# Attention weights turned by 32x32 blocks on DVE and exchanged through DRAM, in place of TensorE transposes

## Chip, cores and metric

One NeuronCore of a Trainium2 chip. The metric is the device time of one execution in microseconds, lower is better; for the kernel before, three runs gave a median of 1193.29 us (1192.71 to 1195.32).

## What is computed

One hybrid decoder layer on x (1, 1024, 1024) in float32: RMSNorm, a projection to six blocks of 512 columns (conv gate b, c, h and attention q, k, v), a causal 3-tap convolution on four blocks of 128 channels, attention on 8 heads of 64, an output projection, and a mixture of 32 experts. The attention is what the change touches. With qk = q k^T after normalising, for each head:

```python
z = einsum('bhqd,bhkd->bhqk', qb, kb) * scale
mask = s_idx < t_idx
log_keep = where(mask, log_sigmoid(-z), 0.0)
shifted = concatenate([log_keep[..., 1:], zeros], axis=-1)
suffix = cumsum(shifted, axis=3, reverse=True)
A = where(mask, exp(log_sigmoid(z) + suffix), 0.0)
out = einsum('bhqk,bhkd->bhqd', A, vb)
```

So each query row's weights A come from a running product along the keys, which the kernel computes with queries on partitions. The product with v sums over keys, so keys must be on partitions there: A has to be turned.

## The kernel before, in words

The kernel is one program in which every engine has a list of instructions written out by hand; semaphores order them. Its first part, functions mix_sp, mix_pool, mix_pe, mix_act and mix_dve, makes the projections, the convolution and the attention. The second part multiplies by w_out, routes the tokens and runs the 32 experts; the change doesn't touch it, though SyncE's requests for x and the expert weights stand in its list behind those of mix_sp.

**Units.** The attention is cut into 32 units: 4 pairs of heads, and in each pair the 8 tiles of 128 queries, longest first. Unit n belongs to pair n // 8, has tile 7 - n % 8 and rows of length (tile + 1) * 128 keys: 1024 for n % 8 = 0, then 896 and so on down to 128. I write r for n % 8. The two heads of a pair are h = 0 and 1, each with buffers soft[h], kept[h], probsT[h] of its own.

**A unit's way.** TensorE makes the scores z (line 471, four PSUM banks for both heads together). ACT (open_unit) reads them twice with a sigmoid, into kept (line 653) and soft (line 654). DVE (weigh) runs a product scan over kept from the right (line 847) and multiplies it into soft (line 850). TensorE turns soft tile by tile with transposes (turn, line 482) into PSUM banks 4 and 5, in groups of four tiles. ACT copies them to probsT (take_turned, line 662). TensorE multiplies by v (values, line 496) into bank 6. After each four units ACT copies bank 6 to y_mix (take_values, line 671), whose rows 0 to 3 hold the convolution's channels and rows 4 to 7 the heads' output.

**Projection in between.** The rest of TensorE's time in this stretch goes to the projection of 20 chunks of 128 columns (project, line 433), in two halves of 512 tokens, called groups, each of 24 matmuls, called ticks. Eight groups come before the first unit; after that SHARE gives each unit of pairs 0 to 2 8 ticks after its first turn and 16 after its second, and SHARE_LAST gives 24 and 24 to the first four units of pair 3 (24 to 27) and none to the last four (28 to 31, from LIGHT on). These groups go to PSUM bank 7 (group_bank), one after the other. ACT or DVE (take) reads them out; semaphores bank_read tell when. The weights of a chunk are loaded by SyncE (load_chunk, line 316), rounded by POOL (chunk_hi, line 366) and their rest made by DVE (chunk_lo, line 790), in two buffers each.

**Order.** TensorE's list for unit n < 28 is: scores(n+1), values(n-1), turn(n, 0), 8 ticks, turn(n, 1), 16 ticks; at r = 4 (JOIN) it also makes sums for the norms. For n >= 28: values(n-1), scores(n+1), both turns, and in units 29 and 30 the first w_out products (first_rows). Behind the units come the sums for the last norms, values(31) and the other first_rows, among them chunk 7 last, which needs the last attention rows normalised. DVE's list has in iteration n: evacuations, weigh(n+1, 0), in each second iteration a chunk_lo, weigh(n+1, 1). ACT's has for each head take_turned(n, h) and open_unit(n+1, h). open_unit waits until the turns of the unit before have read soft[h].

**SyncE** loads x, the small constants and the chunks of w_in, each when the buffer is free, waits for all projections (filled), loads the eight chunks of w_out (line 344), and goes on to x again (line 1251), g2b (1253), more x (1255, 1256), W1 (1257) and the stores of xn2_rows (1260).

```python
            for n in range(LIGHT):
                p, r = divmod(n, NT)
                scores(n + 1)
                if n:
                    values(n - 1)
                turn(n, 0)
                project(ticks_by(n, 0), ticks_by(n, 1))
                turn(n, 1)
```

## Time and profile before

| | us |
|---|---|
| median of three runs | 1193.29 (1192.71 to 1195.32) |
| the profiled execution | 1188.81 |
| its span | 1186.6 |
| TensorE matmuls busy | 1103.5 (93%) |
| DVE busy | 885.8 (75%) |
| ACT busy | 731.3 (62%) |
| POOL busy | 138.9 (12%) |
| matmuls of line 433 in 90 to 500 us | 113.0, 112.5 and 109.4 for the three terms |
| transposes, line 482 | 44.0 for 288 |
| copies to probsT, line 662 | 43.8 for 96 |

The span is the profiled execution from the first to the last instruction; 2.2 us of its time lie around it. TensorE's matmuls are pipelined, so their busy times overlap, and distances between starts say more. All numbers of a profile are of one execution. The granted clock of TensorE over the whole execution was 0.972 of full speed.

### The profile page before, as it was taken

Reading aid. Unit: us, or ns where it says so; the run is one execution under the profiler, and the core shown is the slowest. Engines: PE = TensorE matmul, PEld = TensorE weight load, DVE = VectorE, ACT = ScalarE, POOL = GpSimd, SP = SyncE. Lnnn points to the kernel's source line nnn. Section 1 sums busy time; section 2 is a strip of 40 time slices with the busy share of each in tenths; the row PEclk is TensorE's granted clock in tenths of the full one; section 3 lists DMA queues with packets and bytes.
Section 4 is the critical chain, followed back from the end, with each engine's and each line's share of the span. In section 5 each row is a group of like instructions: output and inputs, shape, how many; then the busy total and the mean of one; then the engine's idle time right before and its main releaser. Section 6 shows DMA issues by size and latency. Waiting matters only on the chain. (4 is left out here: it accounts for less than half of the span.)

```text
span 1186.6 us, 16859 instructions
## 1 busy us (share of the span) xinstructions
PE 1103.5 (93%) x5834; PEld 901.5 (76%) x5834; DVE 885.8 (75%) x1014; ACT 731.3 (62%) x914; POOL 138.9 (12%) x193
## 2 busy tenths in 40 slices
PE   8998999999999989995699999999999999999950
PEld 7886777877778758884588888888888888888840
DVE  5405656666575573567699999999999999999946
ACT  5322655656733482212588888888888888888840
POOL 1001000000010021001001111111111111111000
PEclk9998999999999999997899999999999999999985
DMA  7111001101011054002899999999999999999619
GB/s 232 40 36 36 19 20 35 36 19 36 19 36 37 1 215 193 36 36 110 357 427 404 389 393 384 390 381 380 390 376 380 390 381 380 385 385 382 239 58 386
DMA packets 58459, 261.90 MB, mean 221 GB/s; under 512 B 14128, under 2 KB 34608, under 8 KB 45104
## 3 DMA queue, kind: packets, MB, share of 16 engines
q1 hardware_dynamic: 48048, 240.32, 52.8%
q0 software_dynamic: 9216, 16.80, 3.7%
q10 hardware_dynamic: 1152, 4.19, 0.9%
q8 instruction: 29, 0.48, 0.2%
q14 instruction: 14, 0.11, 0.0%
HBM read 252.89 MB, written 25.17 MB: 234 GB/s over the span
## 5 line engine op out<-in xcount | busy, mean ns | idle before, releaser
L1133 DVE TENSOR_TENSOR e_lo<-W,e_hi 128x1024 fp32r<-128x1024 f32 x384 | 452.2, 1221 | 26.5 <-ACT e_hi L1127 23.7
L1127 ACT ACTIVATE e_hi<-W 128x1024 fp32r<-128x1024 f32 x384 | 403.2, 1060 | 97.4 <-PE ps L1098 88.9
L1096 PE MATMUL ps<-e_hi,xT_hi 128*128 128x512 f32 x512 | 203.4, 397 | 7.5 <-DVE e_lo L1133 5.1
L1098 PE MATMUL ps<-e_lo,xT_hi 128*128 128x512 f32 x512 | 200.4, 391 | 0.0
L1097 PE MATMUL ps<-e_hi,xT_lo 128*128 128x512 f32 x512 | 200.0, 391 | 0.0
L847 DVE TENSOR_TENSOR_SCAN kept<-kept,start_at 128x1024 f32<-128x1024 f32 (+7 forms) x64 | 89.2, 1393 | 56.0 <-ACT kept L653 56.0
L433 PE MATMUL ps<-xnT_hi,w_hi 128*128 128x512 f32 x320 | 128.6, 402 | 2.4 <-DVE y_mix L822 0.9
L433 PE MATMUL ps<-xnT_hi,w_lo 128*128 128x512 f32 x320 | 128.1, 400 | 0.0
L433 PE MATMUL ps<-xnT_lo,w_hi 128*128 128x512 f32 x320 | 125.0, 391 | 0.0
L1096 PEld LDWEIGHTS ps<-e_hi,xT_hi 128*128 128x128 f32 x512 | 97.0, 189 | 27.5 <-DVE e_lo L1133 3.7
L662 ACT ACTIVATE probsT<-ps 128x512 f32<-128x512 f32 (+3 forms) x96 | 43.8, 491 | 112.1 <-PE ps L482 112.0
L1098 PEld LDWEIGHTS ps<-e_lo,xT_hi 128*128 128x128 f32 x512 | 96.5, 189 | 20.7
L1097 PEld LDWEIGHTS ps<-e_hi,xT_lo 128*128 128x128 f32 x512 | 96.7, 189 | 19.0
L1096 PE MATMUL ps<-e_hi,hidT_hi 128*128 128x512 f32 x256 | 102.4, 400 | 2.7 <-DVE e_lo L1133 2.7
L1098 PE MATMUL ps<-e_lo,hidT_hi 128*128 128x512 f32 x256 | 100.0, 390 | 0.0
L1097 PE MATMUL ps<-e_hi,hidT_lo 128*128 128x512 f32 x256 | 99.9, 390 | 0.0
L1193 POOL DMA_INDIRECT y_rows<-y,idx_pair x32 | 32.7, 1022 | 455.4 <-ACT y L1153 455.4
L433 PEld LDWEIGHTS ps<-xnT_hi,w_hi 128*128 128x128 f32 x320 | 60.5, 189 | 16.0 <-issue 3.8
L433 PEld LDWEIGHTS ps<-xnT_hi,w_lo 128*128 128x128 f32 x320 | 60.1, 188 | 12.9 <-issue 0.7
L433 PEld LDWEIGHTS ps<-xnT_lo,w_hi 128*128 128x128 f32 x320 | 60.2, 188 | 12.3 <-issue 0.5
L366 POOL CAST w_hi<-w_raw 128x1024 fp32r<-128x1024 f32 x20 | 22.9, 1145 | 308.9 <-DMA w_raw<-in_w_in_dram 308.9
L1096 PEld LDWEIGHTS ps<-e_hi,hidT_hi 128*128 128x128 f32 x256 | 48.2, 188 | 11.9 <-issue 2.9
(220 smaller groups left out, 1679.9 us busy)
## 6 DMA issues: line engine op xcount, KB each, us to landing
W<-in_w_dram SPq DMA_DIRECT2D x96, 2048.0 KB, 11.6
w_raw<-in_w_in_dram SPq DMA_DIRECT2D x20, 512.0 KB, 3.9
yy<-y_rows SPq DMA_DIRECT2D x8, 1024.0 KB, 13.5
xt<-in_x_dram SPq DMA_DIRECT2D x8, 512.0 KB, 3.9
w_out_raw<-in_w_out_dram SPq DMA_DIRECT2D x8, 512.0 KB, 7.5
xn_rows<-xn SPq DMA_DIRECT2D x8, 512.0 KB, 2.6
out_dram<-x ACTq DMA_DIRECT2D x8, 512.0 KB, 8.9
x<-in_x_dram SPq DMA_DIRECT2D x2, 1536.0 KB, 10.6
```

Of the source, the lines that this page charges most:

```text
L366: pool.tensor_copy(w_hi[c % 2], w_raw[c % 2]).then_inc(w_hi_made, 1)
L433: mm = pe.matmul(ps[:, group_bank(g)], w, r, start=(i % TICKS == 0), stop=(i % TICKS == TICKS - 1))
L662: act.activation(probsT[h][:, k0:k1, :], TB(th(n, h) + hf)[:, 0:(k1 - k0) * P].rearrange("p (k t) -> p k t", t=P), ACT.Copy).then_inc(turn ...
L847: dve.tensor_tensor_scan(back, back, one[:, ::-1], 0.0, ALU.mult, ALU.max).then_inc(multiplied, 1)
L1096: pe.matmul(o, xs_hi[:, k], e_hi[:, p, cols], start=(k == 0), stop=False)
L1097: pe.matmul(o, xs_lo[:, k], e_hi[:, p, cols], start=False, stop=False)
L1098: mm = pe.matmul(o, xs_hi[:, k], e_lo[:, p, cols], start=False, stop=(k == last))
L1127: act.activation(e_hi[:, p], flat[:, p * D:(p + 1) * D], ACT.Copy).then_inc(s["hi_made"], 1)
L1133: dve.tensor_tensor(e_lo[:, p], flat[:, p * D:(p + 1) * D], e_hi[:, p], ALU.subtract).then_inc(s["lo_made"], 1)
L1193: pool.indirect_dma_start(out=y_rows, out_offset=bass.IndirectOffsetOnAxis(ap=idx_pair[b].bitcast(U32), axis=0), in_=y[b], in_offset=None, ...
```

## The change

Each unit's weights are no longer turned by TensorE. DVE transposes them in blocks of 32x32 (a new instruction behind each product), into a free row of y_mix or another free buffer (quads_turned). SyncE stores that buffer to DRAM (spread: one transfer per head) and loads it back with the blocks at their places (collect: four transfers per head, one per group of 32 partitions), as 128 runs of a quarter row each. The turns on TensorE and the copies on ACT are gone. values(n) waits for the collects (exchanged) and reads probsT in four pieces of 32 columns. collect(n) waits for values(n-1), since there is one probsT per head. DVE's transpose of unit n waits for the store of unit n-1.

The two PSUM banks that the turns used, 4 and 5, now take the projection's groups in turn, so a group waits for the evacuation of the group two before it. In SyncE's list the chunk loads from the seventh on stand behind the collect of the unit whose evacuation frees them, and the w_out loads, still behind the wait for all projections, come in twos, each pair of them ahead of the stores and collects of units 28, 29, 30 and 31. POOL's first copies of y_mix also wait for the last store of unit 27.

```diff
@@ -122,7 +123,8 @@
         soft = [at(f"soft{i}", 112 + 4 * i, [P, S]) for i in range(2)]
         kept = [at(f"kept{i}", 120 + 4 * i, [P, S]) for i in range(2)]
         y_mix = at("y_mix", 128, [P, 2 * CB, S])
-        probsT = [at(f"probsT{i}", 160 + 4 * i, [P, NT, P]) for i in range(2)]
+        probsT = [at(f"probsT{i}", 160 + 4 * i, [P, S]) for i in range(2)]
+        turned_end = at("turned_end", 80, [P, S])
         u = at("u", 184, [P, S + TAPS - 1])
         conv_sq = at("conv_sq", 188.125, [P, S])
         q_sq = at("q_sq", 192.125, [P, S])
...
@@ -256,7 +259,7 @@
             return range(ticks_by(n, part) // TICKS, ticks_by(n, part + 1) // TICKS)
 
         assert ticks_by(UNITS - 1, 2) == 2 * len(CHUNKS) * TICKS
-        group_bank = lambda g: 6 + g % 2 if g < PRE_GROUPS else 7
+        group_bank = lambda g: 6 + g % 2 if g < PRE_GROUPS else 4 + g % 2
 
 
         JOIN = (4, 4, 4, 2)
...
@@ -291,8 +294,29 @@
         z_reads = lambda n, h: z_before[n] + (h + 1) * halves(n)
         assert all(z_first[n] % 2 == 0 for n in range(UNITS) if halves(n) == 2)
 
-        th = lambda n, h: sum(2 * halves(m) for m in range(n)) + h * halves(n)
-        TB = lambda g: ps[:, 4 + g % 2]
+        QUAD = 32
+        QUADS = P // QUAD
+
+        def quads_turned(n, h):
+
+            p, r = divmod(n, NT)
+            if h == 0:
+                t = y_mix[:, CB + p]
+            elif p < NPAIR - 1:
+                t = y_mix[:, CB - 1]
+            else:
+                t = turned_end if r < NT // 2 else kept[1]
+            return t[:, 0:length(n)].rearrange("p (b k i) -> p b k i", b=QUADS, i=QUAD)
+
+        def quads(n, h):
+
+            L = length(n)
+            return quad_rows[n % 2, h, 0:P * L].rearrange("(p c) -> p c", c=L)
+
+        def quads_home(n, h):
+
+            return probsT[h][:, 0:length(n)].rearrange("p (a k i) -> p a k i", a=QUADS, i=QUAD)
+
         VB = 6
 
         row_gain = lambda r: gain_conv[:, r:r + 1] if r < CB else gain_attn[:, r - CB:r - CB + 1]
...
@@ -337,11 +361,36 @@
                         sp.dma_start(g2_col, norm_ffn_w.rearrange("a (k p) -> p (a k)", k=KT)).then_inc(router_in, 16)
                     sp.dma_start(router_b[:, 0:NG], b_group.partition_broadcast(P)[:, 0, :]).then_inc(router_in, 16)
                     sp.dma_start(router_b[:, NG:], b_expert.partition_broadcast(P)[:, 0, :]).then_inc(router_in, 16)
-            for c in range(2, len(CHUNKS)):
+            def spread(n):
+                for h in range(2):
+                    sp.wait_ge(turned, 2 * n + h + 1)
+                    sp.dma_start(quads(n, h), quads_turned(n, h).rearrange("p b k i -> p (b k i)")).then_inc(spread_out[h], 16)
+
+            def collect(n):
+                for h in range(2):
+                    sp.wait_ge(spread_out[h], 16 * (n + 1))
+                    if n and h == 0:
+                        sp.wait_ge(valued, n)
+                    for b in range(QUADS):
+                        sp.dma_start(quads_home(n, h)[b * QUAD:(b + 1) * QUAD].rearrange("j a k i -> j a (k i)"),
+                                     quads(n, h).rearrange("(a j) (b r) -> b j a r", a=QUADS, b=QUADS)[b]).then_inc(exchanged[h], 16)
+
+            for c in range(2, PRE + 2):
                 load_chunk(c)
+            for n in range(LIGHT):
+                spread(n)
+                collect(n)
+                if n:
+                    for part in range(2):
+                        for g in groups_in(n - 1, part):
+                            if g % 2 and g // 2 + 2 < len(CHUNKS):
+                                load_chunk(g // 2 + 2)
             sp.wait_ge(filled, 2 * len(CHUNKS))
-            for c in OUT_ORDER:
-                sp.dma_start(w_out_raw[:, c], w_out_v[:, c]).then_inc(w_out_in[c], 16)
+            for n in range(LIGHT, UNITS):
+                for c in OUT_ORDER[2 * (n - LIGHT):2 * (n - LIGHT) + 2]:
+                    sp.dma_start(w_out_raw[:, c], w_out_v[:, c]).then_inc(w_out_in[c], 16)
+                spread(n)
+                collect(n)
         def mix_pool(pool):
             pool.memset(eps, EPS).then_inc(consts_made, 1)
             pool.memset(start_at, 0.0).then_inc(consts_made, 1)
...
@@ -379,6 +428,7 @@
             pool.tensor_tensor(router_w, router_w, g2_col.unsqueeze(2).to_broadcast([P, KT, LOG]), ALU.mult).then_inc(router_scaled, 1)
             pool.wait_ge(scored, NT * (NPAIR - 1))
             pool.wait_ge(rows_scaled, 6)
+            pool.wait_ge(spread_out[1], 16 * LIGHT)
             for m in range(2):
                 for rows in (slice(0, CB - 1), slice(CB, LAST)):
                     pool.tensor_copy(yT_hi[m][:, rows], y_mix[:, rows, m * P:(m + 1) * P]).then_inc(y_hi_made, 1)
...
@@ -424,9 +474,7 @@
                     if i % TICKS == 0:
                         if h == 0:
                             pe.wait_ge(w_lo_made, c + 1)
-                        if PRE_GROUPS <= g:
-                            pe.wait_ge(bank_read[(g - 1) % 2], (g - 1) // 2 + 1)
-                        elif g >= 2:
+                        if g >= 2:
                             pe.wait_ge(bank_read[g % 2], g // 2)
                     w = (w_hi, w_hi, w_lo)[term][c % 2][:, k]
                     r = (xnT_hi, xnT_lo, xnT_hi)[term][:, k, h * BANK:(h + 1) * BANK]
...
@@ -472,20 +520,11 @@
                                            start=(i == 0), stop=(i == 2))
                 mm.then_inc(scored, 1)
 
-            def turn(n, h):
-                pe.wait_ge(weighed, 2 * n + h + 1)
-                for hf in range(halves(n)):
-                    g = th(n, h) + hf
-                    if g >= 2:
-                        pe.wait_ge(turned_read, g - 1)
-                    for j in range(4 * hf, min(4 * hf + 4, length(n) // P)):
-                        mm = pe.transpose(TB(g)[:, (j % 4) * P:(j % 4 + 1) * P], soft[h][:, S - length(n) + j * P:S - length(n) + (j + 1) * P], ident)
-                    mm.then_inc(turned, 1)
-
             def values(n):
 
                 p, t = n // NT, tile_of(n)
-                pe.wait_ge(turned_read, th(n + 1, 0))
+                for h in range(2):
+                    pe.wait_ge(exchanged[h], 16 * QUADS * (n + 1))
                 if n == 0:
                     pe.wait_ge(bank_read[0], PRE)
                 elif n % 4 == 0:
...
@@ -493,7 +532,7 @@
                 for j in range(t + 1):
                     for h in range(2):
                         head = slice((2 * p + h) * HD, (2 * p + h + 1) * HD)
-                        mm = pe.matmul(ps[h * HD:(h + 1) * HD, VB, (t % 4) * P:(t % 4 + 1) * P], v[:, j, head], probsT[h][:, j, :],
+                        mm = pe.matmul(ps[h * HD:(h + 1) * HD, VB, (t % 4) * P:(t % 4 + 1) * P], v[:, j, head], quads_home(n, h)[:, :, j],
                                        start=(j == 0), stop=(j == t))
                 mm.then_inc(valued, 1)
...
@@ -523,9 +562,7 @@
                 scores(n + 1)
                 if n:
                     values(n - 1)
-                turn(n, 0)
                 project(ticks_by(n, 0), ticks_by(n, 1))
-                turn(n, 1)
                 if r == JOIN[p]:
                     if p + 1 < NPAIR:
                         sums_of_qk(p + 1)
...
@@ -540,8 +577,6 @@
                 values(n - 1)
                 if n + 1 < UNITS:
                     scores(n + 1)
-                for h in range(2):
-                    turn(n, h)
                 if n == UNITS - 3:
                     first_rows((0,))
                 if n == UNITS - 2:
...
@@ -646,21 +681,12 @@
                 if n % NT == 0:
                     act.wait_ge(q_minus_made, p + 1)
                 if n:
-                    act.wait_ge(turned, th(n - 1, h) + halves(n - 1))
+                    act.wait_ge(turned, 2 * (n - 1) + h + 1)
                 up, down = q_scale[p % 2][:, t, h:h + 1], q_minus[p % 2][:, t, h:h + 1]
                 b = 2 * h + z_first[n] % 2
                 z = psf[:, b * BANK:b * BANK + L]
                 act.activation(kept[h][:, S - L:], z, ACT.Sigmoid, scale=down).then_inc(kept_made, 1)
                 act.activation(soft[h][:, S - L:S - 1], z[:, 0:L - 1], ACT.Sigmoid, scale=up).then_inc(z_read, halves(n))
-
-            def take_turned(n, h):
-                for hf in range(halves(n)):
-                    act.wait_ge(turned, th(n, h) + hf + 1)
-                    if hf == 0 and n:
-                        act.wait_ge(valued, n)
-                    k0, k1 = 4 * hf, min(4 * hf + 4, length(n) // P)
-                    act.activation(probsT[h][:, k0:k1, :], TB(th(n, h) + hf)[:, 0:(k1 - k0) * P].rearrange("p (k t) -> p k t", t=P),
-                                   ACT.Copy).then_inc(turned_read, 1)
 
             def take_values(i):
...
@@ -725,9 +751,8 @@
                     w_out_round(OUT_ORDER[2:4])
                 if n == LIGHT + 3:
                     w_out_round(OUT_ORDER[4:6])
-                for h in range(2):
-                    take_turned(n, h)
-                    if n + 1 < UNITS:
+                if n + 1 < UNITS:
+                    for h in range(2):
                         open_unit(n + 1, h)
                 if n and n % 4 == 0:
                     take_values(n // 4 - 1)
...
@@ -848,6 +873,10 @@
                 dve.wait_ge(multiplied, 2 * n + h + 1)
                 dve.wait_ge(z_read, z_reads(n, h))
                 dve.tensor_tensor(s[:, :L - 1], s[:, :L - 1], k[:, 1:], ALU.mult).then_inc(weighed, 1)
+                if n:
+                    dve.wait_ge(spread_out[h], 16 * n)
+                dve.wait_ge(weighed, 2 * n + h + 1)
+                dve.transpose(quads_turned(n, h).rearrange("p b k i -> p k b i"), s.rearrange("p (k b i) -> p k b i", b=QUADS, i=QUAD)).then_inc(turned, 1)
 
             def w_out_rest(c):
                 dve.wait_ge(w_out_hi_made, OUT_ORDER.index(c) + 1)
```

## Rows read from the trace of the kernel before

**Rows 1.** Windows: us, each engine's busy us (x instructions), clock, DMA share, GB/s.

```profile
191.68:270.40 78.72, 77.89 (x509) 60.19 (x508) 51.51 (x51) 47.72 (x81) 6.34 (x5) 1.00 0.09 28
...
415.00:445.50 30.50, 24.80 (x156) 16.57 (x155) 23.42 (x34) 23.78 (x41) 7.30 (x17) 1.00 0.57 211
```

**Rows 2.** Groups by line: busy us, mean ns, idle before and its releaser.

```profile
L847 DVE TENSOR_TENSOR_SCAN kept<-kept,start_at 128x1024 f32<-128x1024 f32 (+7 forms) x64 | 89.2, 1393 | 56.0 <-ACT kept L653 56.0
...
L850 DVE TENSOR_TENSOR soft<-soft,kept 128x1023 f32<-128x1023 f32 (+7 forms) x64 | 50.6, 790 | 2.2
...
L433 PE MATMUL ps<-xnT_hi,w_hi 128*128 128x512 f32 x280 | 113.0, 404 | 2.4 <-DVE y_mix L822 0.9 <-DVE u L806 0.7 <-DVE u L811 0.7
```

**Rows 3.** Timeline of TensorE, unit 2: start us, us, engine, instruction.

```profile
142.44 0.39 PE L433 MATMUL ps<-xnT_lo,w_hi 128*128 128x512 f32 x1
142.67 0.81 PE L482 MATMUL ps<-start_at,soft 128*128 128x128 f32 x6
143.24 0.47 PE L433 MATMUL ps<-xnT_hi,w_lo 128*128 128x512 f32 x1
```

**Rows 4.** Timeline of TensorE, units 0 and 1, start of unit 2.

```profile
114.88 0.80 PE L471 MATMUL ps<-k_hi,q_hi 64*128 64x512 f32 x2 [4.23 <-ACT soft L654]
...
119.27 0.59 PE L433 MATMUL ps<-xnT_hi,w_hi 128*128 128x512 f32 x1
119.70 0.40 PE L433 MATMUL ps<-xnT_lo,w_hi 128*128 128x512 f32 x1
...
128.19 1.97 PE L496 MATMUL ps<-probsT,v 128*64 128x128 f32 x32
...
137.25 0.50 PE L471 MATMUL ps<-k_hi,q_hi 64*128 64x512 f32 x2
```

**Rows 5.** Timeline of DVE, second head of unit 0, start of unit 1.

```profile
118.65 2.28 DVE L847 TENSOR_TENSOR_SCAN kept<-kept,start_at 128x1024 f32<-128x1024 f32 x1
120.96 1.23 DVE L850 TENSOR_TENSOR soft<-soft,kept 128x1023 f32<-128x1023 f32 x1
122.11 2.02 DVE L847 TENSOR_TENSOR_SCAN kept<-kept,start_at 128x896 f32<-128x896 f32 x1
```

**Rows 6.** Timeline of TensorE, unit 23 and the start of unit 24.

```profile
341.24 0.50 PE L471 MATMUL ps<-k_hi,q_hi 64*128 64x512 f32 x2
...
342.82 0.66 PE L496 MATMUL ps<-probsT,v 128*64 128x128 f32 x8
...
349.30 0.50 PE L471 MATMUL ps<-k_hi,q_hi 64*128 64x512 f32 x2
```

**Rows 7.** Lines of SyncE: issue ns min/median/max, first to last start; landings.

```profile
L316 SPq DMA_DIRECT2D w_raw<-in_w_in_dram x20: 539/540/672, 8.7 to 381.2; - x20
...
DMA to landing us min/median/max: 3.7/3.9/7.9
...
L327 SPq DMA_DIRECT2D k_gain<-in_k_norm_w_dram x2: 596/882/1167, 20.7 to 22.6; - x2
...
L344 SPq DMA_DIRECT2D w_out_raw<-in_w_out_dram x8: 333/434/457, 415.3 to 418.6; - x8
...
DMA to landing us min/median/max: 3.2/7.5/11.6
...
L1257 SPq DMA_DIRECT2D W<-in_w_dram x1: 537/537/537, 444.5 to 444.5; - x1
...
L1260 SPq DMA_DIRECT2D xn_rows<-xn x8: 319/320/342, 450.9 to 552.5; - x8
...
DMA to landing us min/median/max: 2.6/2.6/9.1
```

**Rows 8.** Timeline of TensorE behind the last projection matmul.

```profile
415.21 1.31 PE L496 MATMUL ps<-probsT,v 128*64 128x128 f32 x20
...
433.33 0.44 PE L496 MATMUL ps<-probsT,v 128*64 128x128 f32 x4 [0.84 <-ACT probsT L662]
...
444.15 0.50 PE L1238 MATMUL ps<-w_out_hi,yT_hi 128*128 128x512 f32 x1 [0.41 <-DVE yT_lo L1231]
```

More of the change, by code:

```diff
@@ L77, in hymba_moe_layer @@
     y_rows = nc.dram_tensor("y_rows", (PAIRS, D), F32, kind="Internal").ap()
+    quad_rows = nc.dram_tensor("quad_rows", (2, 2, P * S), F32, kind="Internal").ap()
     with ExitStack() as ctx:
@@ L230, in hymba_moe_layer @@
         turned = sem("turned")
-        turned_read = sem("turned_read")
+        spread_out = [sem(f"spread_out{h}") for h in range(2)]
+        exchanged = [sem(f"exchanged{h}") for h in range(2)]
         valued = sem("valued")
@@ L559, in mix_pe @@
             pe.wait_ge(end_squared, 3)
-            pe.wait_ge(turned_read, th(UNITS, 0))
+            pe.wait_ge(bank_read[0], len(CHUNKS))
             pe.matmul(ps[:, 4], same_head, last_sq[:, 0:BANK], start=True, stop=True).then_inc(end_summed, 1)
```

## The prediction

> **What bounds the kernel now.** First the windows by stage: from 108.9 us (first attention unit) to 415.1 us (last projection matmul) TensorE is never free; in 191.68 to 270.40, the eight units of head pair 1, it is busy 77.89 of 78.72 us, DVE 51.51 and ACT 47.72 [rows 1]. So a microsecond taken off TensorE there is worth up to one, until another chain takes over. In the stage behind it, 415.0 to 445.5, TensorE is busy 24.80 of 30.50 us and serial steps matter [rows 1]. Then the groups by line, for DVE's scan and product, 64 each, and for what the projection waits for [rows 2]. Then the timelines, for what one turn costs in sequence, and SyncE's issues, since the new path runs over them.
>
> I call the end of the last projection matmul T0: 415.1, just ahead of the values(27) at 415.21 [rows 8].
>
> **TensorE: what goes.** Matmul busy time overlaps, so I take distances between starts: a turn of six tiles lies between 142.67 and the next projection matmul at 143.24 [rows 3]; 0.57 us, 0.10 us a tile. Of the 288 tiles, 30 lie in units 0 and 1 and 20 behind T0 (both costed below); 238 remain: 23.9 us. The second PSUM bank takes away the 2.4 us for which projection matmuls waited on evacuations [rows 2]. Together **-26.3 us** at T0, if all else follows. ACT loses its 96 copies; it was not the bound, so that counts nothing.
>
> **DVE: what comes.** 64 transposes of the sizes of line 850's operands, against 51.51 us of present work in such a pair. I take that line's price (50.6 us in all [rows 2]; a full row holds DVE for 1.15 us, 120.96 to 122.11 [rows 5]), as both read and write 32-bit rows once. A cheap end isn't excluded; at two thirds of that price each long-row start and the head below would lose 0.8 to 1.6 us less, 4 us in the sum. The scan, 89.2 us for the same 64 sizes [rows 2], is the dear end. DVE gets to some 63 of 72 us per pair: no bound on average, but one while rows are long.
>
> **The new chain.** A unit's weights, once turned on DVE, need: two stores, 8 loads (4 per head) on SyncE, then values(n). Rows for an issue: 0.54 us for w_raw, with several runs per partition, at most 0.67; 0.33 to 0.46 us for w_out, one run per partition; 0.60 to 1.17 us for k_gain's single numbers [rows 7]. A collect has runs in two dimensions, as w_raw has; with 0.03 between two I take **0.57 us per collect**; ends 0.37 (an isolated single-run issue) and 0.88 (k_gain's middle). Landing: a 512 KB store lands in 2.6 us from its issue [rows 7]; I use 2.6 for stores and collects alike. Hence:
> (a) last turned to usable: 0.35 + 2.6 + 3 x 0.57 + 2.6 = 7.2 us;
> (b) collect(n) may not start before values(n-1) is done (probsT has one buffer): 7 x 0.57 + 2.6 + 0.2 = 6.8 us from one values to the next.
>
> Head. DVE ends the second product of unit 0 at 122.11 [rows 5]; two transposes more make 124.4, usable at 131.6 by (a). Before, values(0) ran at 128.19 [rows 4]. TensorE arrives at about 125 and idles 6 us; after the 4.23 us gap at 114.88 it ran at its lower level (1.2 GHz) until 119.70: 119.27 to 119.70 is one step of 0.43, where 142.44 to 142.67 is one of 0.23 [rows 3, 4]. 4.8 us at half pace cost 2.4. Unit 2 begins at 131.6 + 1.9 (values) + 5.8 (24 projection steps of 0.23 and the changes of operand) + 2.4 = 141.7, before 137.25 [rows 4]: **+4.4** (bounds 2.5 to 6).
>
> Long rows, at the start of pairs 1 and 2 (pair 3's units have 48 ticks and cover it). DVE per head: 3.46 (118.65 to 122.11) + 1.15 = 4.6 us at 1024 [rows 5], and at 896, with a scan of 2.02 and two steps of 1.0, 4.1; so with w_lo (as a product, 1.14) and an evacuation (0.7) the iterations that open units r=0 and r=1 take 9.3 and 10.0 us. TensorE needs only 7.7 each without turns: 341.24 to 349.30 less 0.4 of turns [rows 6]. Counting from scores of r=0 (time 0), DVE is done at 12.3 and 22.4, usable 19.5 and 29.6; TensorE wants them at 16.7 and then at 28.4. Stalls 2.9 + 1.2, twice: **+8.1** (bounds 6 and 11).
>
> Other units: between two values lie 5.8 us of projection and 0.5 to 1.4 of scores [rows 6], 6.3 to 7.2 in all, against 6.8 by (b). Only the two shortest wait, 0.3 and 0.4: **+2** over three pairs (bounds 0 and 12). The w_raw loads, now behind a collect, are late by under a unit, and a chunk has two units; the copies of w_raw and the router's stay covered.
>
> At T0: -26.3 + 4.4 + 8.1 + 2 = **-11.8 us**.
>
> **Behind T0: the new wait.** SyncE waits for all projections before w_out, then issues per unit: two w_out loads (1 MB), two stores, 8 collects. Everything behind stands in that order. w_out's landings rise from 3.2 to 11.6 us over 8 loads issued 0.47 apart [rows 7]: 1.67 us per 512 KB. A store behind them waits for them: the first xn_rows store, issued at 450.9 behind W (2 MB, issued 444.5, with 2.5 MB of x ahead of it), took 9.1 us to land instead of 2.6 [rows 7]. So from a unit's first w_out issue to its first store's landing: 3.2 + 1.67 + 0.8 (256 KB) = 5.7 us, then 5.5, 5.3, 5.1 for shorter rows; then 8 x 0.57 = 4.6. Four units: 21.6 + 18.2 = 39.8, plus 2.0 to the last landing: values(31) at T0 + 41.8. Before: 433.33, T0 + 18.2 [rows 8]. **+23.6**. The turned blocks themselves are ready (each unit's DVE work is under 5 us), so SyncE's order sets this.
> From values(31) to the first w_out product of the last chunk it was 10.9 us (to 444.15 [rows 8]), partly behind w_out rounds on ACT, which are done by then: about 8.4 now, **-2.5**. The chunks (4, 5, 2, 6, 3) still fit beside it.
> The x rows are requested 21 us later than before but land by T0 + 48, before their use at T0 + 50. Later stages just shift.
>
> **Sum:** -11.8 + 23.6 - 2.5 = **+9.3 us** on the profiled execution: 1188.81 to 1198.1. That execution lies 4.5 below the median of the runs, 1193.29; on the median I forecast **1203 us**.
>
> A page's rule and a row. The w_raw load (512-byte runs, 512 KB) lands in 3.9 us, the xn_rows store of the same bytes in 4 KB runs in 2.6 [rows 7]: small runs cost some 1.3 us per 512 KB, and a unit's collects, spread over 4.6 us of issues, hide that. The Trainium skill ("DMA: Bandwidth & Descriptors", Measured) says that transfers under 64 KB are dominated by descriptors and gives 0.95 us of transfer for 64 KB; collects served one by one at that would make the sum about +70 us, an estimate from that page. The rule speaks for the third rival below.
>
> **Rivals.**
> 1. *Faster: issues are cheap.* If an 8-fold burst of collects costs no more than the isolated 0.33 + 0.04, the same working gives (a) 6.3, (b) 5.4: head +3.5, long rows +6, others 0, so -16.8 at T0; behind it 8 x 0.37 per unit, +15: total -2. If issues cost nothing beside the landings, -19.8 and +4: -16, 1177 us. The deciding point is a pace of 0.41 us. For: the collects are small. Against: every multi-run issue in the rows is 0.54 or more, and back-to-back ones are dearer than isolated ones. Chance 14%.
> 2. *The 32x32 transpose is slow on DVE*, like the scan: 39 us more on DVE. Each long-row start loses 5 more, the head 3: +22, 1216 us. For: no row shows this operation. Against: it needs no recurrence. 12%.
> 3. *Collects are paced by transfer or by dear issues*, 0.88 us each: (b) becomes 9.0, above every unit's own 6.3 to 7.2: +31 at T0 and +31 behind: some +60, 1255 us. For: 256 small transfers. Against: the rows on w_raw. 6%.
> 4. *w_out doesn't hold up the stores*, if stores overtake loads: 2.2 us less per unit, 8.8 in all: total +0.5, 1194. For: they are other transfers, to another memory. Against: the xn_rows landing. 6%.
>
> **Numbers.** Forecast (+2.5 to +22) 62%. Range: from rival 1's and 4's nearer ends, -4, to +29 (upper bounds of issue pace, 0.68, with rival 2): **1189 to 1222**. A measurement tells 0.2% (2.4 us) from nothing. Faster 0.14; within, 0.08 (most of rival 4, the low edge of the forecast); slower 0.78.
>
> **What the profile would show.** Right: no line-482 work; DVE transposes near 1.2 us for 1024; TensorE near 71 us per pair in the middle of the run but stalls of 1 to 6 us on the collects in units 1, 9, 10; T0 about 12 us earlier; values(31) some 42 us behind T0, with three or four TensorE gaps of 6 to 9 us and a lower granted clock in them; SyncE busy issuing. Wrong: collects issued below 0.41 us apart, a transpose above 1.5 us, stores landing in 2.6 us behind w_out, or T0 later than before.

## The result, and the profile after

Median 1258.62 us (four runs, 1252.60 to 1260.22) against 1193.0 for the kernel before on the same chip: ratio 1.053, 95% interval 1.050 to 1.057. The forecast was 1203, the range 1189 to 1222. Direction right, size far off. The profiled execution took 1260.22 us (before 1188.81), its span 1258.0 (1186.6): 71.4 us more. Two distances divide them: T0, the last projection matmul, moved from 415.2 to 459.1 (+43.9; forecast -11.8), and from there to the end the kernel takes 27.5 us more (forecast 23.6 - 2.5 = 21.1).

Windows of the kernel after: head pair 1 (from its second scores to those of pair 2), the whole stretch up to T0, the stage behind T0. They answer to [rows 1].

```profile
202.06:297.61 95.55, 75.77 (x437) 58.18 (x438) 61.90 (x67) 38.44 (x57) 5.52 (x5) 0.89 0.42 122
...
108.90:459.10 350.20, 290.26 (x1639) 223.83 (x1638) 232.01 (x239) 135.38 (x193) 20.47 (x19) 0.90 0.42 124
...
459.00:499.00 40.00, 16.79 (x95) 10.84 (x94) 21.26 (x33) 16.16 (x25) 3.12 (x4) 0.69 0.58 173
```

The pair takes 95.6 us where it took 78.7. TensorE was the bound; now it is idle a fifth of the time, and its granted clock is 0.89 instead of 1.00. DVE, busy 61.9 of 95.6 us, isn't the bound either. When no engine is full, look for a ring of waits.

Groups by line of the kernel after, 90 to 560 us, by form for the transposes (columns as in [rows 2]):

```profile
L481 PE MATMUL ps<-xnT_hi,w_hi 128*128 128x512 f32 x280 | 118.6, 423 | 3.3 <-DVE w_lo L815 3.3
...
L535 PE MATMUL ps<-probsT,v 128*64 128x128 f32 x576 | 52.2, 342 | 67.8 <-DMA probsT<-quad_rows 55.7 <-issue 12.1
L875 DVE TENSOR_TENSOR soft<-soft,kept 128x1023 f32<-128x1023 f32 (+7 forms) x64 | 50.6, 790 | 2.2
...
L879 DVE STREAM_TRANSPOSE y_mix<-soft 128x1024 f32<-128x1024 f32 x7 | 8.7, 1245 | 0.6
...
L879 DVE STREAM_TRANSPOSE y_mix<-soft 128x128 f32<-128x128 f32 x7 | 2.2, 312 | 0.7
```

The transposes cost what the products cost: 64 of them, 49.8 us together (43.6 into y_mix, 4.2 into turned_end, 2.0 into kept) against 50.6. That term was right. Most of TensorE's idle time stands ahead of values: 67.8 us, 55.7 of them put down to the collects and 12.1 to nothing that the profile shows. The waits of 90 to 560 us say who else waits:

```profile
POOL w_hi L415 <- DMA w_raw<-in_w_in_dram: 306.4, 16, 39.4
DVE w_lo L815 <- POOL w_hi L415: 101.0, 15, 9.6
ACT kept L688 <- DVE y_mix L879: 82.4, 28, 10.7
```

In the kernel before, DVE's wait for w_hi ahead of chunk_lo came to 7.0 us in three waits, longest 3.2. Now DVE stands still 101.0 us in 15, for a load. Which load that is, is seen in the timeline of the kernel after, the collect of unit 2 and DVE's work on unit 3:

```profile
144.73 3.64 SPq L375 DMA_DIRECT2D probsT<-quad_rows  x8
145.37 0.83 DVE L875 TENSOR_TENSOR soft<-soft,kept 128x639 f32<-128x639 f32 x1
146.30 0.85 DVE L879 STREAM_TRANSPOSE y_mix<-soft 128x640 f32<-128x640 f32 x1
148.42 0.56 SPq L340 DMA_DIRECT2D w_raw<-in_w_in_dram  x1
149.02 10.40 SPq L367 DMA_DIRECT2D quad_rows<-y_mix  x2
...
153.55 1.04 POOL L415 CAST w_hi<-w_raw 128x1024 fp32r<-128x1024 f32 x1 [39.44 <-DMA w_raw<-in_w_in_dram]
154.62 1.22 DVE L815 TENSOR_TENSOR w_lo<-w_raw,w_hi 128x1024 fp32r<-128x1024 f32 x1 [7.48 <-POOL w_hi L415]
155.77 1.48 DVE L872 TENSOR_TENSOR_SCAN kept<-kept,start_at 128x640 f32<-128x640 f32 x1
157.28 0.82 DVE L875 TENSOR_TENSOR soft<-soft,kept 128x639 f32<-128x639 f32 x1
158.21 0.84 DVE L879 STREAM_TRANSPOSE y_mix<-soft 128x640 f32<-128x640 f32 x1
...
159.52 4.10 SPq L375 DMA_DIRECT2D probsT<-quad_rows  x8
```

Unit 2's collect holds SyncE to 148.37; behind it the chunk load is issued, lands by 153.5, POOL rounds it, DVE makes w_lo. Only then can DVE weigh and turn the second head of unit 3, store it and let the collect begin. TensorE's values(3) starts at 165.36, 6.27 us idle. The next load (171.52) stands behind the collect of unit 4, and that one behind this collect. This is a ring, closed once in two units: **collect, load, w_hi, w_lo, second head, store, collect**. The kernel before had the same chunk at DVE 10 us earlier, and the load after it shows how short the way was:

```profile
144.66 1.22 DVE L790 TENSOR_TENSOR w_lo<-w_raw,w_hi 128x1024 fp32r<-128x1024 f32 x1
...
156.28 0.54 SPq L316 DMA_DIRECT2D w_raw<-in_w_in_dram  x1
...
160.21 1.51 POOL L366 CAST w_hi<-w_raw 128x1024 fp32r<-128x1024 f32 x1 [17.87 <-DMA w_raw<-in_w_in_dram]
162.06 1.21 DVE L790 TENSOR_TENSOR w_lo<-w_raw,w_hi 128x1024 fp32r<-128x1024 f32 x1
```

From the load's issue to its use by DVE lie 5.8 us, and POOL's part ends 0.34 us before DVE begins. There was no cover of two units.

SyncE's lines of the kernel after (collects, stores, chunk loads; each with the landings printed for it), against [rows 7]:

```profile
L375 SPq DMA_DIRECT2D probsT<-quad_rows x256: 302/432/1623, 125.0 to 496.6; - x128
DMA to landing us min/median/max: 1.6/2.1/4.9
...
L340 SPq DMA_DIRECT2D w_raw<-in_w_in_dram x20: 540/546/666, 8.6 to 437.7; - x20
...
DMA to landing us min/median/max: 3.8/4.5/7.9
```

Eight collects in a row take 3.64 us, 0.455 each, in unit 2 (96 KB each) as in units 28 to 31 (64 to 16 KB); I had taken 0.57. The Trainium skill ("DMA: Bandwidth & Descriptors", Measured) gives 0.95 us for one transfer of 64 KB; served one by one, eight would take 7.6 us, an estimate from that page. The trace shows that they aren't served one by one: the issues follow each other without a gap and the transfers overlap.

Behind T0, TensorE and SyncE, against [rows 8]:

```profile
459.13 1.31 PE L535 MATMUL ps<-probsT,v 128*64 128x128 f32 x20
...
470.52 1.98 PE L535 MATMUL ps<-probsT,v 128*64 128x128 f32 x16 [9.35 <-DMA probsT<-quad_rows]
...
480.90 1.55 PE L535 MATMUL ps<-probsT,v 128*64 128x128 f32 x12 [5.54 <-DMA probsT<-quad_rows]
...
489.51 1.12 PE L535 MATMUL ps<-probsT,v 128*64 128x128 f32 x8 [4.11 <-DMA probsT<-quad_rows]
498.55 0.70 PE L535 MATMUL ps<-probsT,v 128*64 128x128 f32 x4 [4.21 <-DMA probsT<-quad_rows]
```
```profile
468.94 0.91 SPq L391 DMA_DIRECT2D w_out_raw<-in_w_out_dram  x2
469.89 0.43 SPq L367 DMA_DIRECT2D quad_rows<-y_mix  x1
470.36 0.43 SPq L367 DMA_DIRECT2D quad_rows<-kept  x1
475.10 3.64 SPq L375 DMA_DIRECT2D probsT<-quad_rows  x8
478.78 0.91 SPq L391 DMA_DIRECT2D w_out_raw<-in_w_out_dram  x2
```

SyncE goes round once per 9.8 us: loads, stores, 4.3 us of waiting for them, collects. values(31) is 39.4 us behind T0 (forecast 41.8).

### The profile page after: what moved, and what is told of

Its sections match the earlier page's. It is cut to its first block and busy times, and to the rows that moved or that the text cites. A ratio compares the mean times of both kernels' runs of the same rounds, so it can differ in the third digit from the quotient of the medians.

```text
span 1258.0 us, 16563 instructions
## 1 busy us (share of the span) xinstructions
PE 1105.6 (88%) x5546; PEld 900.0 (72%) x5546; DVE 929.8 (74%) x1078; ACT 694.8 (55%) x818; POOL 137.4 (11%) x193
## 5 line engine op out<-in xcount | busy, mean ns | idle before, releaser
L688 ACT ACTIVATE kept<-ps,q_minus 128x1024 f32<-128x1024 f32 (+7 forms) x64 | 47.5, 742 | 178.4 <-DVE y_mix L879 82.4
L481 PE MATMUL ps<-xnT_hi,w_hi 128*128 128x512 f32 x320 | 134.1, 419 | 3.3 <-DVE w_lo L815 3.3
L481 PE MATMUL ps<-xnT_lo,w_hi 128*128 128x512 f32 x320 | 129.7, 405 | 0.0
L815 DVE TENSOR_TENSOR w_lo<-w_raw,w_hi 128x1024 fp32r<-128x1024 f32 x20 | 24.9, 1245 | 123.6 <-POOL w_hi L415 123.6
L535 PE MATMUL ps<-probsT,v 128*64 128x128 f32 x576 | 52.2, 342 | 67.8 <-DMA probsT<-quad_rows 55.7
L535 PEld LDWEIGHTS ps<-probsT,v 128*64 128x64 f32 x576 | 42.9, 175 | 76.8 <-issue 76.0
L872 DVE TENSOR_TENSOR_SCAN kept<-kept,start_at 128x1024 f32<-128x1024 f32 (+7 forms) x64 | 86.4, 1350 | 12.5 <-ACT kept L688 12.5
L481 PEld LDWEIGHTS ps<-xnT_hi,w_hi 128*128 128x128 f32 x320 | 63.3, 198 | 23.9 <-issue 7.3
L481 PEld LDWEIGHTS ps<-xnT_hi,w_lo 128*128 128x128 f32 x320 | 63.1, 197 | 14.7 <-issue 0.7
```

The lines of the kernel that those rows point to most:

```text
L481: mm = pe.matmul(ps[:, group_bank(g)], w, r, start=(i % TICKS == 0), stop=(i % TICKS == TICKS - 1))
L535: mm = pe.matmul(ps[h * HD:(h + 1) * HD, VB, (t % 4) * P:(t % 4 + 1) * P], v[:, j, head], quads_home(n, h)[:, :, j], start=(j == 0), stop= ...
L688: act.activation(kept[h][:, S - L:], z, ACT.Sigmoid, scale=down).then_inc(kept_made, 1)
L815: dve.tensor_tensor(w_lo[c % 2], w_raw[c % 2], w_hi[c % 2].bitcast(F32), ALU.subtract).then_inc(w_lo_made, 1)
L872: dve.tensor_tensor_scan(back, back, one[:, ::-1], 0.0, ALU.mult, ALU.max).then_inc(multiplied, 1)
```

## The experiments

**Theory A** (the ring): the chunk load behind a collect delays DVE between the heads. **Theory B**: the exchange itself, with one probsT and one SyncE list, sets the time, wherever the load stands. Times are medians, with the ratio to the kernel before on the same chip; T0, read as the start of values(27), and values(31) are of the profiled execution.

| kernel | us | ratio (95%) | T0 | values(31) |
|---|---|---|---|---|
| before | 1193 | | 415.2 | T0 + 18.1 |
| after | 1258.6 | 1.050 to 1.057 | 459.1 | + 39.4 |
| e1 loads first | 1214.2 | 1.017 to 1.021 | 417.1 | + 39.3 |
| e2 w_lo behind both heads | 1222.0 | 1.022 to 1.027 | 425.8 | + 39.5 |
| e3 before, late load alone | 1237.1 | 1.035 to 1.040 | 460.3 | + 20.0 |
| e4 w_out issued by ACT | 1256.2 | 1.050 to 1.057 | 457.7 | + 39.0 |
| e6 before, transposes alone | 1214.0 | 1.010 to 1.022 | 436.2 | + 19.6 |
| e7 exchange left out | 1167.9 | 0.976 to 0.982 | 386.9 | + 20.2 |
| e8 loads issued by POOL | 1202.0 | 1.006 to 1.011 | 406.0 | + 39.7 |
| b1 before, loads by POOL | 1192.0 | 0.997 to 1.001 | 416.6 | + 18.1 |
| e9 exchange from n % 8 = 2 | 1186.5 | 0.991 to 0.997 | 410.2 | + 19.9 |
| e10 exchange to unit 27 | 1196.8 | 1.001 to 1.005 | 419.9 | + 19.7 |
| e11 exchange from n % 8 = 3 | 1195.8 | 0.999 to 1.003 | 420.4 | + 18.7 |
| e12 as e9, two banks in pair 3 | 1176.3 | 0.984 to 0.989 | 397.1 | + 20.6 |

**e1: the loads ahead of the exchange in SyncE's list.**

```diff
             for n in range(LIGHT):
-                spread(n)
-                collect(n)
                 if n:
...
                                 load_chunk(g // 2 + 2)
+                spread(n)
+                collect(n)
```

> The changed kernel with each w_raw load ahead of the stores and collects of its unit instead of behind them. Theory A (the late chunk load closes a ring: collect(n), w_raw load, w_hi, w_lo between the two heads on DVE, second head's weigh, store, collect(n+1)): DVE's wait for w_hi falls from 101 us to under 15, T0 from 459 us to 400 to 412, time to 1200 to 1212 us. Theory B (the exchange itself, with one probsT buffer and one SyncE list, is too slow for a unit): T0 moves by under 10 us, time 1248 to 1260.

1214.2 us, T0 42 us earlier. DVE's waits for w_hi between 90 and 460 us fell from 101.0 us to 4.3 in three:

```profile
DVE w_lo L815 <- POOL w_hi L415: 4.3, 3, 3.4
```

The order of two entries in one list was worth 44 us, two thirds of the loss. A holds, though T0 (417.1) and the time lie 5 and 2 us above the ranges that it gave; B is out.

**e2: DVE makes w_lo behind both heads**, everything else as in the kernel after: the ring is cut at another link.

```diff
...
+                weigh(n + 1, 1)
                 if n:
                     for g in groups_in(n - 1, 1):
...
-                weigh(n + 1, 1)
```

> The changed kernel with DVE's w_lo behind the second head's weigh instead of between the heads; the load stays where the change put it. Theory A: the ring is cut, though DVE still waits some 2 us for w_hi in each second unit: T0 at 412 to 432, time 1212 to 1232 us. Theory B: under 10 us of change, 1248 to 1260.

1222.0. DVE still waits for w_hi, 54.5 us in 12, but with the weights of both heads already stored. The late load costs little where no one is queued behind its wait, as A has it, though not nothing: TensorE then meets w_lo itself (6.7 us of its matmuls' waits, in two).

**e3: the kernel before, its turns and all, but each chunk load from the seventh on waits until DVE has weighed the first head of unit n+1**, about where the changed kernel issues it.

```diff
-            for c in range(2, len(CHUNKS)):
+            for c in range(2, PRE + 2):
                 load_chunk(c)
+            for n in range(1, LIGHT):
+                for part in range(2):
+                    for g in groups_in(n - 1, part):
+                        if g % 2 and g // 2 + 2 < len(CHUNKS):
+                            sp.wait_ge(weighed, 2 * (n + 1) + 1)
+                            load_chunk(g // 2 + 2)
```

> The kernel before (turns on TensorE, no exchange) with the w_raw loads from the seventh on held until DVE has done the first head of the unit whose iteration uses them, about when the change issues them. Theory A: DVE waits 5 to 7 us for w_hi in each of some 13 iterations, and as TensorE's second turn comes late in the unit, half of it or less reaches TensorE: 1200 to 1235 us. Theory B: the loads have two units of slack, no change: 1190 to 1195.

1237.1, T0 +45.1, with no exchange at all, and 2 us over the top of A's range. B can't give that. A line of DVE's waits, and of TensorE's groups up to T0:

```profile
DVE w_lo L796 <- POOL w_hi L372: 78.4, 15, 6.3
```
```profile
L439 PE MATMUL ps<-xnT_hi,w_hi 128*128 128x512 f32 x258 | 109.4, 424 | 26.3 <-DVE q_lo L808 11.3 <-DVE y_mix L828 7.0 <-DVE u L812 5.9
```

Here the delay reaches TensorE mostly through the one projection bank: the evacuations by DVE stand behind the stalled w_lo. That path is not the changed kernel's, which has two banks and loses the time ahead of values, so the 45.1 us show that a late load is dear, not by which way it was dear in the changed kernel.

**e7: the kernel after without stores and collects**, its chunk and w_out loads in SyncE's list as in the kernel before. values reads the blocks where DVE wrote them, in two buffers in turn; what is left out is the exchange between partition groups, so the output isn't the layer's.

```diff
-                for h in range(2):
-                    pe.wait_ge(exchanged[h], 16 * QUADS * (n + 1))
+                pe.wait_ge(turned, 2 * n + 2)
...
-                        mm = pe.matmul(ps[h * HD:(h + 1) * HD, VB, (t % 4) * P:(t % 4 + 1) * P], v[:, j, head], quads_home(n, h)[:, :, j],
+                        mm = pe.matmul(ps[h * HD:(h + 1) * HD, VB, (t % 4) * P:(t % 4 + 1) * P], v[:, j, head], quads_turned(n, h)[:, :, j],
```

> The changed kernel without stores and collects: the values product reads the turned blocks where DVE wrote them, in two buffers per head, so blocks of other partition groups are multiplied and the attention's output is not the reference's; chunk and w_out loads stand as in the kernel before. This is the change with an exchange that costs nothing. By the prediction's own terms T0 falls by 24 to 28 us and the tail keeps its length: 1163 to 1170 us. If the DVE order or the projection holds TensorE up even so: 1180 to 1200.

1167.9, T0 -28.3. My first sum was -26.3: turns and the bank give what they were said to give.

**e8: the kernel after with the chunk loads issued by POOL** (0.88 us an issue there), where nothing stands ahead of them but POOL's own work on the chunk before.

> The changed kernel with all w_raw loads issued by POOL, just ahead of its own copy of each chunk, so SyncE has only stores and collects. Theory A: DVE's wait for w_hi under 15 us, T0 at 400 to 412 us, 1200 to 1212 us; the collects' latency in long rows (two or three stalls per pair, each followed by matmuls at the lower clock) remains. If SyncE's own order was all there was to it, T0 falls to 390 to 400 and the time to 1190 to 1200.

1202.0, T0 406.0. DVE still waits 19.9 us for w_hi, where under 15 was expected. That is the forecast's own case: without the late load the working gives 1203, T0 -11.8, values(31) + 41.8; measured 1202.0, -9.2, + 39.7. That the median fits to 1 us is partly luck: the profiled execution is 13.2 us over that of the kernel before, forecast 9.3, and T0 and values(31) behind it miss in opposite directions. The starts of the long rows came as forecast, in the first unit of pairs 1 and 2:

```profile
206.31 3.68 PE L531 MATMUL ps<-probsT,v 128*64 128x128 f32 x32 [4.70 <-issue]
...
284.34 3.68 PE L531 MATMUL ps<-probsT,v 128*64 128x128 f32 x32 [4.43 <-issue]
```

That is 9.1 us of waiting, where 2.9 + 1.2 twice (8.1) were forecast, all of it in the first unit and none in the second; each time values then runs at the lower clock (3.68 us against 1.97).

TensorE's values up to T0, in the kernel after and in e8:

```profile
L535 PE MATMUL ps<-probsT,v 128*64 128x128 f32 x516 | 45.5, 338 | 44.5 <-DMA probsT<-quad_rows 32.5 <-issue 12.1
```
```profile
L531 PE MATMUL ps<-probsT,v 128*64 128x128 f32 x516 | 39.2, 305 | 14.9 <-issue 12.7 <-DMA probsT<-quad_rows 2.0
```

With the waits for scores (12.0 and 7.3) and for w_lo (3.3 and 0) TensorE stands still 59.8 us in the one and 22.2 in the other: 37.6. And it is busy 290.1 us from 109 to 459 in the one, 274.8 from 109 to 406 in the other: 15.2 less for the same work, at a granted clock of 0.95 instead of 0.90. 52.8 together, for a T0 that differs by 53.1. The Trainium skill ("DMA: Bandwidth & Descriptors", Issuing engines are not separate DMA queues) says that issuing from another engine saves only the sequencer's time. Here the other queue's issue is dearer, 0.88 against 0.55 us, and it still gained 57 us: what moved was the load's place behind a waiting instruction.

**b1, the control: the kernel before with the loads on POOL.** Nothing else differs from before.

> Control: the kernel before with nothing changed but the queue of the w_raw loads, POOL instead of SyncE. In the kernel before the loads were never late, so both theories expect no difference over 3 us: 1190 to 1196. If it is faster by more, the gain of the mixed kernels is partly that of the queue.

1192.0, no difference, as expected: the queue matters only where something waits in it.

**e4: w_out issued by ACT** in units 28 and 29, so that SyncE's tail list holds stores and collects alone.

```diff
-            sp.wait_ge(filled, 2 * len(CHUNKS))
...
-                for c in OUT_ORDER[2 * (n - LIGHT):2 * (n - LIGHT) + 2]:
-                    sp.dma_start(w_out_raw[:, c], w_out_v[:, c]).then_inc(w_out_in[c], 16)
...
+                if n in (LIGHT, LIGHT + 1):
+                    for c in OUT_ORDER[4 * (n - LIGHT):4 * (n - LIGHT) + 4]:
+                        act.dma_start(w_out_raw[:, c], w_out_v[:, c]).then_inc(w_out_in[c], 16)
```

> The changed kernel with the eight w_out loads issued by ACT, four each in units 28 and 29, so that SyncE's stores and collects don't stand behind them. If w_out in front costs each of the last four units 2 to 3 us, values(31) moves from T0 + 39.4 to T0 + 29 to 33 and the time to 1247 to 1253 us. If it costs nothing there (DVE, the landings or the bandwidth set the pace): values(31) within 3 us of T0 + 39, 1255 to 1261.

1256.2, no gain. TensorE behind T0 in e4:

```profile
477.17 1.98 PE L532 MATMUL ps<-probsT,v 128*64 128x128 f32 x16 [17.48 <-DMA probsT<-quad_rows]
484.50 1.13 PE L532 MATMUL ps<-probsT,v 128*64 128x128 f32 x12 [2.12 <-DMA probsT<-quad_rows]
490.77 0.66 PE L532 MATMUL ps<-probsT,v 128*64 128x128 f32 x8 [1.80 <-DMA probsT<-quad_rows]
496.65 0.44 PE L532 MATMUL ps<-probsT,v 128*64 128x128 f32 x4 [1.93 <-DMA probsT<-quad_rows]
```

Three rounds fall to 5.9 to 7.3 us, but the first grows from 9.4 to 17.5 us of waiting. ACT issued all eight loads within 4.7 us (461.70 to 466.41), and the collects of unit 28, issued in the same stretch, landed late; the kernel after has a median of 2.1 us:

```profile
L375 SPq DMA_DIRECT2D probsT<-quad_rows x8: 378/436/678, 461.5 to 464.8; - x8
...
DMA to landing us min/median/max: 1.9/8.4/12.2
```

The stores of unit 29, issued at 466.64 and 468.75 behind the eight loads but on another queue, took 11.4 and 9.6 us to land. So the bytes of w_out are paid, not only their place in the list; this speaks against rival 4.

**e6: the kernel before with the 64 transposes added on DVE**, into the same spare buffers, read by no one; open_unit waits for them as in the changed kernel.

> The kernel before, turns on TensorE and all, plus the 64 transposes on DVE into spare room, each behind its product; nothing reads them. If DVE's own time for them (49 us) has room beside TensorE: 1190 to 1203 us (the long rows may cost some). If DVE becomes the bound by them: 1215 to 1240.

1214.0, between the two ranges (up to 1203, and from 1215): 49.8 us of DVE work put 21.0 on T0, though DVE has room on average. TensorE up to T0 in e6:

```profile
L449 PE MATMUL ps<-xnT_hi,w_hi 128*128 128x512 f32 x256 | 106.3, 415 | 12.9 <-DVE u L828 4.0 <-DVE u L823 4.0 <-DVE y_mix L839 3.8
```

Before, this line waited 2.4 us. The 10.5 us more are the half of the 21.0; most of the rest is slower matmuls (TensorE busy 307.5 us up to T0 against 298.1, granted clock 0.96 against 0.99). The one bank is emptied mostly by DVE, which now reaches an evacuation up to 1.2 us later for each transpose ahead of it. In e7 the same transposes run with two banks, and the first term waits 0.0 us. So the second bank is worth more than the 2.4 us at which I had it: it is the cover of the transposes.

**e9 to e11: which units should be exchanged.** The kernel before with loads on POOL, one projection bank, the last four units (and in e9 and e11 the longest rows) still turned by TensorE. ex(n) chooses; the rest follows it.

```diff
+        ex = lambda n: n < LIGHT and (n >= 3 * NT or n % NT >= 2)
...
             def turn(n, h):
+                if ex(n):
+                    return
```

> The kernel before, with the 32x32 blocks and the exchange only where a unit's rows are short or its successor's projection is long: units with n % 8 of 2 and more in pairs 0 to 2, and units 24 to 27; the other 6 units and the last four (28 to 31) are still turned by TensorE. One PSUM bank for the projection as before, w_raw loads issued by POOL, w_out loads in one block as before. 178 of the 288 tiles leave TensorE (17.8 us). Theory (exchange pays where its 7 us lie beside other work; the loss of the changed kernel was the late load, the long-row starts and the tail): T0 at 397 to 405 us, a tail of 18 to 19 us, 1173 to 1185 us in all, faster than both kernels. Rival (every unit's exchange and DVE's added transposes lengthen the chain, as the transposes alone did in the kernel before, +21 us): T0 at 412 to 430, 1190 to 1210.

> As the run with n % 8 of 2 and more, but all of units 0 to 27 are exchanged and only units 28 to 31 are turned by TensorE. This is the changed kernel with the loads on POOL and without its tail (and with one projection bank instead of two). Theory: T0 as in the changed kernel with the loads on POOL, 406, plus up to 4 for the single bank, so 406 to 411, and then a tail of 18 to 20: 1180 to 1190 us. If the tail's cost isn't the exchange, the tail stays near 39 us and the time is 1200 or more.

> As the run with n % 8 of 2 and more, but from n % 8 = 3 on (units 24 to 27 as well). 142 of 288 tiles leave TensorE (14.2 us). Theory: if unit 2's, 10's and 18's exchanges were already hidden, this one is slower than that run by their 36 tiles, 3 to 4 us; if they stall TensorE (the rival for 768-key rows), it is faster than it by up to 5.

e9, 1186.5, beats both kernels, but misses what was expected: 1173 to 1185, T0 410.2 where 397 to 405 was expected. e10, 1196.8, lies over its 1180 to 1190. Its tail is + 19.7: the tail's 21 us are those of the exchange between the w_out loads, and go with it. Its T0, 419.9, is 14 us behind e8's, where up to 4 was expected for the missing bank. e11, with 36 more tiles on TensorE, lost 9.3 us where 3 to 4 were expected. What they have in common is in TensorE's first projection term up to T0: it waits on DVE's evacuations for 12.2 us in e9, 20.0 in e10, 17.3 in e11, and 0.0 in e8, which has two banks. Why e11, with fewer transposes on DVE, waits 5 us more than e9 isn't shown. For e10 and e9:

```profile
L483 PE MATMUL ps<-xnT_hi,w_hi 128*128 128x512 f32 x258 | 107.1, 415 | 20.0 <-DVE y_mix L882 6.5 <-DVE u L866 6.5 <-DVE u L871 5.8
```
```profile
L483 PE MATMUL ps<-xnT_hi,w_hi 128*128 128x512 f32 x256 | 104.8, 409 | 12.2 <-DVE u L871 5.7 <-DVE y_mix L882 3.2 <-DVE u L866 3.0
```

**e12: e9 with two banks in pair 3**, where no turn needs bank 4.

```diff
-        group_bank = lambda g: 6 + g % 2 if g < PRE_GROUPS else 7
+        TWO_BANKS = ticks_by(3 * NT, 0) // TICKS
+        group_bank = lambda g: 6 + g % 2 if g < PRE_GROUPS else 7 if g < TWO_BANKS or g % 2 else 4
```

> As the mixed run from n % 8 = 2 (1186.5 us), with one thing more: in pair 3, where units 24 to 27 are exchanged and no turn uses banks 4 and 5, the projection's groups take banks 4 and 7 in turn. In the mixed run, pair 3 up to T0 took 69.5 us (values(23) at 340.73, values(27) at 410.24) with TensorE busy 60.3 of 69.0 us and waits on evacuations ahead of groups; with two banks in the changed kernel with the loads on POOL the same stretch took 56.6 us. Theory (a single bank's waits, made longer by the DVE time of scan, product and transpose ahead of an evacuation, are what pair 3 lost): T0 at 397 to 402, 1173 to 1180 us. Rival (pair 3's stretch follows DVE's chain and not the bank): T0 at 407 or later, 1183 to 1188.

1176.3, ratio 0.987 (0.984 to 0.989), within what was expected: 82 us better than the change as made. TensorE's first term in it, and a window over pair 3:

```profile
L487 PE MATMUL ps<-xnT_hi,w_hi 128*128 128x512 f32 x256 | 103.4, 404 | 3.5 <-DVE u L872 1.5 <-DVE u L877 1.5 <-DVE y_mix L888 0.2
```
```profile
341.00:399.00 58.00, 58.00 (x340) 45.66 (x340) 46.47 (x45) 22.06 (x27) 7.68 (x8) 1.00 0.47 140
```

TensorE is never free there. From values(23), 340.5, to values(27), 397.1, it takes 56.6 us; e9 took 69.5.

## Why the prediction was wrong, point by point

**The step that failed**, as it stood: "The w_raw loads, now behind a collect, are late by under a unit, and a chunk has two units; the copies of w_raw and the router's stay covered." I priced it at nothing. The first half is true. The cover isn't there: I measured the slack to TensorE's use of the chunk, two units on, and not to the next instruction in the chain, DVE's w_lo, which stands between the two heads of the very next iteration. The trace of before had it: 5.8 us from issue to use. Taken away, the late load gives back 53.1 us of T0 (e8) or 42.0 (e1); added alone to the kernel before, it costs 45.1, by another way (e3).

**TensorE -26.3:** right; -28.3 with a free exchange (e7). The tiles' part is rounded up: 0.57 us for six are 0.095 a tile, which for 238 gives 22.6, not 23.9. And within the sum the bank's 2.4 us was mis-sized: with the transposes on DVE, one bank costs some 10 to 20 us of waits (e6, e10), and 13 to 14 us of T0 (e8 to e10, e9 to e12). Since the change brings both, the error cancelled, which is luck.

**Transposes on DVE at the product's price:** right, 1.245 us for 1024 against 1.22 for the product, and DVE is held 1.16 us (123.40 to 124.56) against 1.15. Rival 2 falls.

**Collect pace 0.57:** 0.455. Close to rival 1's turning point of 0.41 but above it, and other places made up for it. (Rival 1's own (a) is mis-added: 0.35 + 2.6 + 3 x 0.37 + 2.6 are 6.7, not 6.3.) From the last transpose of unit 0, ended at 124.65, to values(0) at 132.33 lie 7.7 us, against 7.2 by (a). The collects of unit 3, for which TensorE stood waiting, began at 159.52 and gave values(3) at 165.36: 5.8, against 6.8 by (b).

**Head +4.4:** right; unit 2 begins at 141.72, forecast 141.7. The 6 us of idling came in two pieces, 3.22 ahead of the second scores at 126.69 (for ACT, which waits for the transpose) and 3.35 ahead of values(0). **Exchange in all up to T0**, +14.5 forecast (4.4 + 8.1 + 2), +19.1 measured (e7 to e8). From 109 us to T0 TensorE is idle 22.2 us in e8 and 8.8 in e7: 13.4 more, where 12.1 of the 14.5 were idling. The other 5.6 are slower matmuls (busy 274.8 against 269.2 us): the waits' effect on the clock, for which I had allowed only in the head.

**Behind T0:** values(31) at + 39.4, forecast + 41.8: right, and SyncE's order and w_out's bytes make it. The closeness owes something to two misses that cancel: from unit 29's first w_out issue to its first collect it is 6.2 us (468.94 to 475.10), forecast 5.5, and its collects take 3.6, forecast 4.6.

**Rival 3** named 1255 us and the result was 1259, but by another way: collects paced 0.88 apart. They were 0.455 apart, and 57 of the 66 us came from a load. A number that fits is no proof of its mechanism.

The parts, from runs: free exchange -28.3, exchange +19.1, late loads +53.1, together +43.9 at T0 (each is the step from one kernel to the next, so they must add up); the stage behind it 27.5 more, of which 21.3 are values(31)'s delay against T0 (39.4 less 18.1). The other 6.2 us lie behind values(31), for which I had forecast a gain of 2.5: from there to the end it is 759.4 us against 753.3 before. But e1 and e8, with the same program behind T0, take 754.2 and 754.5. So about 1 us goes with the change, and the gain of 2.5 didn't come; the other 5 are in this execution of the changed kernel alone, and another execution of it took 7.6 us less in all (1252.60 against 1260.22). Why executions differ by that is open.

## What to carry to other kernels

When a transfer is moved behind a wait in an in-order list, measure its slack to the first instruction that reads its result on any engine, then ask what is queued behind that instruction; here 5.8 us, not two units. An engine with room on average still needs a buffer between it and the bound (a second bank) before work is added to it. And a change that loses as a whole may win in part: exchanged only where 7 us of latency lie beside other work, with the second bank where it is free, it gave 1.3% over the kernel before.

## What the runs showed of the hardware

- A wait costs TensorE more than its length. In the stretch 459 to 499 the granted clock was 0.69. In the kernel after, values(0), 32 matmuls, took 3.68 us behind 3.22 and 3.35 us of idling, against 1.97 in [rows 4]; the granted clock was 0.50 from 126.6 to 136.0, the lower of the two levels, 1.2 GHz. In sum, 37.6 us of idling came with 15.2 us of slower matmuls (after against e8).
- Where nothing held it up, SyncE issued a collect each 0.455 us at every size from 16 to 96 KB, though each has runs in two dimensions; the w_raw issue took 0.546. The number of dimensions alone doesn't tell the price of an issue.
- Stores of 64 KB to 512 KB landed in 1.5 to 6.5 us, median 3.0. Behind w_out loads they took longer whichever engine issued the loads: 192 KB landed in 5.2 us behind two on SyncE (after) and in 11.4 and 9.6 behind eight on ACT (e4).
